# Low parts of the weight tiles placed one step later, and first products taken feature by feature behind three norms

## What is computed

```python
def swiglu_2(h, w_in, w_out):
    g, u = jnp.split(h @ w_in, 2, axis=-1)
    return (jax.nn.silu(g) * u) @ w_out

# block one
u = modulate(rmsnorm(h, g_norm_ffn1), sh1, sc1); h = h + 0.5 * gt1 * swiglu(u, ...)      # w1
u = modulate(rmsnorm(h, g_norm_mix), sh2, sc2);  h = h + gt2 * token_mixing(u, ...)      # wpqk, wv, wg, wbr, wo
u = modulate(rmsnorm(h, g_norm_ffn2), sh3, sc3); h = h + 0.5 * gt3 * swiglu(u, ...)      # norm n2, w2
x = rmsnorm(h, g_final)                                                                 # norm nf
# block two, layer 0: FFN (f0), gMLP (gv, gu, go), FFN (f1); layer 1: FFN (f2), attention (aqk, av, ao), FFN (f3)
x_lat = ffn_sublayer(...); x_ctx = ffn_sublayer(...)        # each ends in a layer norm
```

## Time and profile before

| | |
|---|---|
| median of three runs | 2620.17 us (2618.76 to 2622.85) |
| the profiled execution | 2622.8 us |
| its span | 2621.0 us |
| PE busy | 2491.6 us (95%), 15574 matmuls |
| DVE busy | 1863.1 us (71%) |
| ACT busy | 1104.2 us (42%) |
| mean granted clock of PE | 0.973 |
| loaded from HBM | 450.04 MB, 172 GB/s over the span |

### The profile page before, as it was taken

The page is one execution under the profiler, slowest core; times in us unless marked ns, Lnnn a source line. Parts: engine busy times, 40 slices in busy tenths (PEclk is TensorE's granted clock), DMA queues, the critical chain, the costliest instruction groups (busy, mean ns, idle before and its releaser), DMA issues.

```text
span 2621.0 us, 39392 instructions
## 1 busy us (share of the span) xinstructions
PE 2491.6 (95%) x15574; PEld 2253.0 (86%) x15574; DVE 1863.1 (71%) x3600; ACT 1104.2 (42%) x1650; POOL 0.2 (0%) x4
## 2 busy tenths in 40 slices
PE   4998999989999999999999999999999999998998
PEld 3998989889989888787888898888998888877998
DVE  6987977778879545677887569897785444576656
ACT  3444565444453323734223572222552222645443
POOL 0000000000000000000000000000000000000000
PEclk8998999989989999999999999999999999898999
DMA  8986756758858432454443166676374332222663
GB/s 305 310 265 196 257 193 200 253 179 262 294 182 260 138 97 65 157 181 133 145 147 124 63 188 206 193 233 193 97 269 133 113 105 94 72 66 76 189 187 104
DMA packets 161383, 453.68 MB, mean 173 GB/s; under 512 B 17712, under 2 KB 21296, under 8 KB 161200
## 3 DMA queue, kind: packets, MB, share of 16 engines
q1 hardware_dynamic: 161200, 451.16, 53.4%
HBM read 450.04 MB, written 1.05 MB: 172 GB/s over the span
## 4 chain that ended last, share of the span: by engine, by line
PE 61%; DVE 4%; ACT 3%; issue 1%; DMA 0%; ACTq 0%; SPq 0%; DVEq 0%
PE PS L1116 19%; PE PS L1117 19%; PE PS L1118 19%; PE PS L1258 1%; ACT own L1323 1%; DVE own L1586 1%; PE PS L1141 1%; PE PS L1143 1%; PE PS L1304 0%; DVE X L1682 0%; DVE X L1568 0%; PE PS L1287 0%; ACT NT L1382 0%; DVE Ul L1686 0%; ACT Uh L1378 0%
## 5 line engine op out<-in xcount | busy, mean ns | idle before, releaser
L1586 DVE TENSOR_TENSOR own<-raw,own 128x1024 fp32r<-128x1024 f32 x425 | 518.3, 1221 | 315.2 <-ACT own L1323 312.9
L1116 PE MATMUL PS<-Uh,own 128*128 128x256 f32 (+1 forms) x2064 | 658.1, 319 | 44.4 <-DVE Ul L1671 22.5
L1117 PE MATMUL PS<-Ul,own 128*128 128x256 f32 (+1 forms) x2064 | 645.2, 313 | 0.0
L1118 PE MATMUL PS<-Uh,own 128*128 128x256 f32 (+1 forms) x2064 | 644.9, 312 | 0.0
L1323 ACT ACTIVATE own<-raw 128x1024 fp32r<-128x1024 f32 x425 | 443.1, 1053 | 343.4 <-PE PS L1118 311.0
L1116 PEld LDWEIGHTS PS<-Uh,own 128*128 128x128 f32 x2064 | 399.3, 193 | 77.5 <-issue 37.2
L1117 PEld LDWEIGHTS PS<-Ul,own 128*128 128x128 f32 x2064 | 400.9, 194 | 20.0 <-issue 0.2
L1118 PEld LDWEIGHTS PS<-Uh,own 128*128 128x128 f32 x2064 | 400.6, 194 | 20.2
L1116 PE MATMUL PS<-Hh,own 128*128 128x256 f32 (+1 forms) x1096 | 351.1, 320 | 5.0 <-DVE Hl L1818 3.6
L1117 PE MATMUL PS<-Hl,own 128*128 128x256 f32 (+1 forms) x1096 | 345.9, 316 | 0.0
L1118 PE MATMUL PS<-Hh,own 128*128 128x256 f32 (+1 forms) x1096 | 345.8, 316 | 0.0
(11 more groups left out here) (221 smaller groups left out, 3887.0 us busy)
## 6 DMA issues: line engine op xcount, KB each, us to landing
MODS<-in_mm SPq DMA_DIRECT2D x168, 256.0 KB, 3.6
SCR<-in_mm SPq DMA_DIRECT2D x136, 256.0 KB, 3.6
raw<-in_f0i SPq DMA_DIRECT2D x64, 512.0 KB, 3.7
raw<-in_f1i SPq DMA_DIRECT2D x56, 512.0 KB, 3.6
raw<-in_f2i SPq DMA_DIRECT2D x56, 512.0 KB, 3.5
SCR<-in_ma SPq DMA_DIRECT2D x88, 256.0 KB, 5.4
raw<-in_w1i SPq DMA_DIRECT2D x44, 512.0 KB, 4.6
raw<-in_w2i SPq DMA_DIRECT2D x44, 512.0 KB, 4.3
```

Source lines behind the costliest of these rows:

```text
L1116: e.matmul(o, ll, rh, start=start, stop=False)
L1117: e.matmul(o, lh, rl, start=False, stop=False)
L1118: return e.matmul(o, lh, rh, start=False, stop=stop)
L1586: e.tensor_tensor(low, raw[:, w.n % RING, :], high.bitcast(F32), ALU.subtract).then_inc(s["wlo"].tell(w.n), 1)
```

## The change

The "split" is cut in two. "high" is the ACT copy, put where the split was. "low" is the DVE subtraction with the load behind it. It is put by a new `low_parts`, which runs at the start of the next `chunk`, and after the products in `project`, `wide` and `out_tile`, so that the low part stands behind the DVE work of the step during which its high part is made. Second, behind the norms n2, nf and l11 the first three chunks (gate 0, up 0, gate 1) are taken together: for each feature tile k, PE does the nine matmuls of the three chunks, into three banks. Their ACT and DVE work follows once all eight features are done. If the filler is empty, the three chunks are called (and what they split is put) ahead of the norm's tiles, otherwise behind them. Third, `deep` stays set during the last slab's out products where only one stream runs. Fourth, the mod rate in the first slabs of f0 goes from 1.6 to 0.5 (the 2.4 from the third slab on is as before), and a `flush` ahead of f0 is gone.

```diff
+    def low_parts(self):
+        while self.highs:
+            self.put("low", n=self.highs.pop(0))
+            self.fetch()
...
-        self.put("split", n=n)
-        self.fetch()
+        self.put("high", n=n)
+        self.highs.append(n)
...
     def chunk(self, name, i, lead=LEAD):
         n = len(self.stream)
         self.stream.append((name, i))
+        self.low_parts()
         while self.split <= min(n + lead, self.total - 1) and self.split_next():
             pass
         assert self.split > n
         for _ in range(2 if self.deep else 0):
             self.split_next()
+        if n in self.highs:
+            self.low_parts()
         self.background()
...
     def tallied(self, r, eps, fills):
         self.norming = True
+        self.low_parts()
...
+    def norm_tiles(self, what, site, t, r, fills, after, tiles=None, **fields):
+        first = self.feature_tiles(*tiles) if tiles and not self.filler else None
         for k in range(KT + 1):
             self.put(what, st=site, k=k, n=t["n"], r=r, after=after, **fields)
...
+            if first and k:
+                self.products(first, k - 1)
...
+        if tiles and not first:
+            first = self.feature_tiles(*tiles)
+            for k in range(KT):
+                self.products(first, k)
+        return first
...
+    def feature_tiles(self, st, names):
+        first = len(self.stream)
+        for i, (name, j) in enumerate(names):
+            self.chunk(name, j, LEAD - i)
+        self.low_parts()
+        for i in range(len(names)):
+            self.used[first + i] = ("feature", first + i)
+        return dict(st=st, r=LAT, n=first, banks=tuple(self.bank(True) for _ in names))
...
+    def begin_ffn(self, st, t):
+        j = self.pairs
+        self.pairs += 2
+        self.of_feature("gate", t, 0, st + "i", f=0, j=j)
+        self.of_feature("up", t, 1, st + "i", f=0, j=j)
+        self.hidden(st, 0, slots_of(SLABS)[0], j, t["r"])
+        self.of_feature("gate", t, 2, st + "i", f=1, j=j + 1)
+        self.gated[st, 1, t["r"]] = j + 1
...
         w = self.put(what, st=st, n=n, r=r, bank=self.bank(), **fields)
         self.used[n] = (w.id, 0)
+        self.low_parts()
...
         n = len(slabs) - 1
-        self.deep = False
         if r is BOTH:
+            self.deep = False
             self.outer_halves(st, w_out, firsts[n], slabs[n], n + at, [slots[f] for f in slabs[n]], norm)
         else:
             yield from out(n, norm)
+            self.deep = False
...
-    p.norm_tiles("fin", "nf", t, LAT, (2, 1), w2_last)
+    p.begin_ffn("f0", p.norm_tiles("fin", "nf", t, LAT, (2, 1), w2_last, p.ffn_tiles("f0")))
     for k in range(KT):
         p.put("finscale", k=k)
-    p.rate = 1.6
+    p.rate = 0.5
     p.fill(1000)
-    p.flush()
...
+                elif w.what == "products":
+                    for i, b in enumerate(w.banks):
+                        on.wait_ge(s["wlo"], w.n + i)
+                        if w.k == 0:
+                            claim(b)
+                        u_ready(w.st, w.k, w.r)
+                        m = three(PS[:, b[0], lo:hi], *weights(w.n + i, w.k), Uh[:, w.k, lo:hi], Ul[:, w.k, lo:hi],
+                                  w.k == 0, w.k == KT - 1)
+                        if w.k == KT - 1:
+                            m.then_inc(s["matmul"].tell(("feature", w.n + i)), 1)
```

More of the change, by code:

```diff
@@ L375, in norm_tiles, with rms @@
         self.norming = False
-    def rms(self, site, which, sec, gain, fills, after, ahead=0):
+        if tiles and not first:
[3 more added lines that the diff above has]
+        return first
+    def rms(self, site, which, sec, gain, fills, after, ahead=0, tiles=None):
         if not ahead:
@@ L385, in rms, with layer_norm @@
         self.mod_until(which, sec)
-        self.norm_tiles("rms", site, t, LAT, fills, after, q=which, f=sec)
-    def layer_norm(self, site, l, i, ll, sec, r, keep, fills, after):
+        return self.norm_tiles("rms", site, t, LAT, fills, after, tiles, q=which, f=sec)
+    def layer_norm(self, site, l, i, ll, sec, r, keep, fills, after, tiles=None):
         t = self.tallied(r, 1e-5, fills)
@@ L396, in layer_norm @@
         self.column((site, "s"), "shift", w, sec)
-        self.norm_tiles("ln", site, t, r, fills, after, q=w, f=sec, slab=li)
+        first = self.norm_tiles("ln", site, t, r, fills, after, tiles, q=w, f=sec, slab=li)
         if not keep:
-            return
+            return first
         if li not in self.scaled:
@@ L405, in layer_norm, with products, of_feature, ffn_tiles @@
             self.later(1 + k // 3, lambda k=k: self.put("rescale", st=site, k=k, r=r, slab=li))
+        return first
+    def feature_tiles(self, st, names):
[6 more added lines that the diff above has]
+        return dict(st=st, r=LAT, n=first, banks=tuple(self.bank(True) for _ in names))
+    def products(self, t, k):
+        self.put("products", k=k, **t)
+    def of_feature(self, what, t, i, st, **fields):
+        self.put(what, st=st, n=t["n"] + i, r=t["r"], bank=t["banks"][i], after=("feature", t["n"] + i), **fields)
+        self.held.discard(t["banks"][i][0])
+    def ffn_tiles(self, st):
+        return (st, [(st + "i", 0), (st + "i", FT), (st + "i", 1)])
+    def begin_ffn(self, st, t):
[6 more added lines that the diff above has]
+        self.gated[st, 1, t["r"]] = j + 1
     def project(self, name, i, st, what, r, **fields):
@@ L543, in through, with product_key @@
         return w
+def product_key(w):
+    return w.after or (w.id, 0)
 def schedule(total):
@@ L1144, in tensor @@
                              stop=w.final, skip_group_check=True).then_inc(s["matmul"].tell(("sums", w.n, w.k)), 1)
+                elif w.what == "products":
[8 more added lines that the diff above has]
+                            m.then_inc(s["matmul"].tell(("feature", w.n + i)), 1)
+                elif w.what in ("gate", "up", "pool_in", "qk1") and w.after:
+                    pass
                 elif w.what in ("gate", "up", "pool_in", "qk1", "sigmoid", "gu", "qk2"):
@@ L1318, in scalar @@
                 b = w.bank[0]
-                if w.what == "split":
+                if w.what == "high":
                     on.wait_sem(s_raw[w.n % RING], 16 * (w.n // RING + 1))
@@ L1400, in scalar @@
                 elif w.what == "gate":
[L1401 removed]
+                    on.wait_ge(s["matmul"], product_key(w))
                     if w.j >= 2:
@@ L1582, in vector @@
                     on.wait_sem(s_vecs, 16)
-                elif w.what == "split":
+                elif w.what == "low":
                     on.wait_ge(s["whi"], w.n)
```

32 lines of the change are left out of this document (19 added, 13 removed).

## The result

The changed kernel takes 2576.95 us (median of four runs, 2574.88 to 2579.55); the kernel before, run beside it, 2621.34. The ratio is 0.9831 (95% interval 0.9818 to 0.9843): 44 us less. The forecast was 2605, with a range down to 2594. The direction was right; the gain was 2.7 times the 16.3 us of the sum, and lies outside the range.

The account below looks back on a forecast made before the run. The prediction took PE, busy for 95% of the span, to bound the kernel. Its terms summed to -16.3 us: 2606.5 against the profiled execution, 2603.9 against the median, the middle taken as 2605, range 2594 to 2617.

Parts of the forecast that it names:

- Third, the waits: Whole span: DVE waits 312.9 us for high parts, mostly worth nothing, since PE waits only 7.3 for low parts.
- Features: Products by feature behind n2, nf, l11: -11.8 us; fifth chunk's wait +3.5; at l11 a pair ahead of the tiles +1.15.
- The longer `deep`: In w2's last slab four low parts cost +1.2 us (0 to 3); nf is spared the fifth chunk's wait.
- nm: Before nm, DVE adds before it subtracts, so the last add starts near 240.5, not 244.40: -4.0 us (-2 to -5).
- c01, c10: Between the norm tiles of c01 and c10, DVE's waits at low parts go: -2.5 and -2.0 us.
- wv and attention, gates: Context start beside wv, mods ahead of low parts: +1 us (-1 to +3); mixer's gates, low part behind `branch`: +1 (-2 to +5).
- gv and gu: At gv, PE's waits for low parts between two norms: -1 us (0 to -4); nothing for gu.
- wo to nf: From wo to nf, low parts one step later gain 0.7 us before n2, nothing for nf.
- Mod rate: At the start of f0, the lower rate takes two mods in three out: -1.4 us (0 to -3).
- low parts are late: Rival: low parts late in all four mixer rounds and behind norms, gain of nm, c01, c10 lost: 2634 us; 8%.
- the second part does nothing: Rival: another chain ends as late, so the five terms of the later low parts are 0: 2616 us; 15%.
- the clock stays low through the products: Rival: behind n2, nf and l11 all 72 matmuls run at 0.213 us, +13.5: 2618.5 us, no change; 7%.

Follow-up runs that it names:

- e7: Changed kernel with one more chunk split ahead of the first silu behind n2, nf and l11 (the fifth chunk): 2573.5 us.
- e18: Changed kernel without the longer `deep` (set False ahead of the last slab's out, as before the change): 2581.6 us.
- e2: Changed kernel with the products behind n2, nf and l11 tile by tile as before: 2584.3 us.
- e11: Changed kernel with low parts put right behind their high parts in the last slabs and norm tiles of c01, c02 and c10 alone: 2583.0 us.
- e5: Changed kernel with low parts put right behind their high parts from the start of wv to the end of the first attention alone: 2583.0 us.
- e9: Changed kernel with low parts put right behind their high parts in the mixer's four gate rounds alone: 2581.0 us.
- e10: Changed kernel with low parts put right behind their high parts from c00 to the last slab but one of go alone: 2584.8 us.
- e1: Changed kernel with each low part, and the next chunk's load, put right behind its high part again everywhere: 2613.5 us.

## Why the forecast was wrong

**The step that failed** is "Third, the waits" in "What bounds the kernel": PE waits only 7.3 us for low parts, "the 313 us count only where DVE's lateness reaches PE. One place is the last slab before a norm." The first half is right. But I looked for that lateness under one producer's name and in the norms. It reached PE as X in the attention, as hidden parts at wo, as norm tiles, as the first mixes: 36.6 us for the step that my sum gave 8.9. That is 27.7 us more, of the 28.1 between the gain and the sum; since the parts overlap, so near a fit is in part luck.

By its terms:

- **Features**: -12.7 for the 72 matmuls (forecast -11.8), 22, 16 and 21 slow ones (24), a count that has some luck in it: nf had 27 in e7 and e18. The fifth chunk +3.5 by e7 (+3.5). l11's pair +1.13 by its first wait (+1.15). Net -8.1 so worked out, -7.3 by e2, forecast -7.15. The mechanism held, and the size within what can be told.
- **The longer `deep`**: it costs 1.0 in w2's last slab (1.2), but without it a low part ahead of nf's tiles costs as much, so the term was at nothing in effect. The forecast had the products behind nf without a wait, and `deep` is what keeps them so: 4.3 us are lost when it goes.
- **nm**: 5.4 (4.0). My layout of that chain held: the last add starts at 240.50, forecast near 240.5. **c01, c10**: 6.0 with c02 (4.5); c01's wait for its tile fell from 2.68 to 1.5, and is 2.7 again in e11. It did not go altogether, as I had it.
- **wv and attention, gates**: forecast to lose 1 each, they gain 6.0 and 4.1. Wrong in sign. I laid the new order's delay on what the old order had shown, and gave the old order's pause in front of its low part there (0.52 us in the earlier trace rows) no weight against it.
- **gv and gu**: 1 against 7.8. DVE's 5 us pause up to 1211 is one row of the kernel before, and I had not looked there. **wo to nf**: 0.7 against 5.4.
- **Mod rate**: 1.4 (0 to 3) against 2.5.

Of the rivals, "low parts are late" is refuted: in the stages where it was put the old order is the slower one (e5, e9, e10, e11), and PE's wait of 9.4 us for low parts is under the 20 of its sign; "the second part does nothing" falls by e1, and "the clock stays low through the products" by the stretches above. The Trainium skill, page "TensorE: Matmul & The Clock Gate", section "A second HAM failure mode: psum-queue depth-cycling", tells of a kernel that oscillated between its two clocks, and was set against the change. Here products change bank every three matmuls, and behind the first 22 at n2 the clock was 1.00 for all 75 matmuls of 533.9 to 542.7, of which 50 are by feature. My witness against it was misread: the pause of 1.25 us ends at 801.81, so most of it lies behind the stretch of 767 to 801 us, and not in it. The clock was at 1.00 from 800 to 803 us too.

**How much is the clock?** Over the span, the matmuls started at 0.50 are worth 366 of 256 columns before and 203 after (of 512 columns counted double, of 128 half), the difference 163 x 0.094 = 15 us of the 44; for the low parts' step alone (e1 against the changed kernel) 80 x 0.094 = 7.5 of 36.6. I had no term for stretches that vanish. The rest is PE's shorter waits. The Trainium skill, page "TensorE: Matmul & The Clock Gate", section "HAM oscillation — how this bites in real kernels", puts the penalty at half of the throttled time. In the traces the stretches at 0.50 fell from 142 to 85 us in all, so that rule would give an estimate of 29 us, twice what the count gives. The count shows why: at 0.213 us each, the columns started in those stretches take 366 x 0.213 = 78 of the 142 us and 43 of the 85, and for most of the rest PE had nothing to run.

Open: 1.9 us of the low parts' step are in no stage that was tried (l11 among them), which is no more than the medians can tell. Single stretches at 0.50 come and go between executions (384 to 387 us is there in the changed kernel and not in e7), so no term below some 1.5 us, an estimate from these, is settled.

## What to carry to other kernels

Where an in-order engine waits much and the critical engine seldom waits for the waiting instruction, ask what stands behind it, and look for the critical engine's waits on any product of that engine, a freed PSUM bank too. Put work that may be late behind work that is wanted, everywhere at once. Before filling a pause to hold the clock, or feeding PE more per feature, check that DVE has room in the chunks behind it: behind nm it had none (busy for 44.05 of 45 us), and behind n2, nf and l11 it had (40.0 of 50, 33.7 of 50 and 26.4 of 42).

## What the hardware showed that I had not expected

- Matmuls of no use held the granted clock at 1.00 through a 5.7 us wait and gave back 1.4 to 2.1 us per norm; behind nm, with three matmuls per feature of 0.92 us, they gave at most 0.5.
- A matmul of 128x128 `ones` in plain fp32 shows as two records and takes 0.225 us, nearly twice the 0.12 of 128x256 in fp32r.
- Pauses of about 1 us in the attention of the changed kernel: the one up to 351.4 left the clock at 1.00, and behind those up to 360.5 and 363.0 it was 0.50 from 363.2. In e7 the pauses are the same (0.79, 0.73, and 1.43 near 382 us), and it was 1.00 through the whole attention.
